# Reordering the beginning of a fused two-block transformer kernel: transfers in another order, a first group of six output tiles, and the lent PSUM banks given to a group's last tiles

## The reference

```python
# first block, for l in 0, 1 (stages 0 to 3)
h = concat(meta_tokens, x)                          # 272 x 1024
u = rms_norm(h, norm_mix_pre[l])
a_q, a_k, a_v, b_q, ..., gates = split(u @ w_in[l]) # 1024 -> 8416 columns
o_a = diff_attention(a_q, a_k, a_v, ..., rel_bias_table)   # four branches
o_b, o_c, o_d = gated linear attention, latent attention, windowed attention (also rel_bias_table)
merged = sum over branches of (o @ w_branch) * sigmoid(gates)
h = h + rms_norm(merged @ w_out[l], norm_mix_post[l])
h = h + rms_norm(conv_ffn(rms_norm(h, norm_ffn_pre[l])), norm_ffn_post[l])
# second block (stages 4 to 10)
x = x + 0.5 * swiglu_ffn(x, ...)      # stage 4, then 6, 7, 9
x = x + mixer(x)                      # stage 5: retention and dilated; stage 8: stick-breaking
return rms_norm(x, final_norm)
```

## Time and profile before

| | |
|---|---|
| median of 3 runs | 2211.29 us (2211.26 to 2211.96) |
| the profiled execution, its own time | 2209.07 us |
| its span | 2207.3 us |
| TensorE busy with matmuls | 2168.1 us, 98% of the span |
| VectorE busy | 1513.9 us, 69% |
| ScalarE busy | 1195.3 us, 54% |
| GpSimd busy | 293.4 us, 13% |
| granted TensorE clock, mean over the span | 0.998 |

### The profile page before, as it was taken

The page is one execution under the profiler, slowest core; times in us unless marked ns, Lnnn a source line. Parts: engine busy times, 40 slices in busy tenths (PEclk is TensorE's granted clock), DMA queues, the critical chain, the costliest instruction groups (busy, mean ns, idle before and its releaser), DMA issues.

```text
span 2207.3 us, 43398 instructions
## 1 busy us (share of the span) xinstructions
PE 2168.1 (98%) x17591; PEld 2086.1 (95%) x17591; DVE 1513.9 (69%) x2614; ACT 1195.3 (54%) x2053; POOL 293.4 (13%) x273
## 2 busy tenths in 40 slices
PE   7999999999999999999999999999999999999998
PEld 6989989999998999899999999889999999989998
DVE  5776676887478576779856665677665665886654
ACT  4555456665546555566655444455445444665443
POOL 1000112000110001220002220002210220232211
PEclk9999999999999999999999999999999999999999
DMA  7334435455643354454554655335555555435554
GB/s 239 113 128 139 134 115 177 130 178 173 216 124 115 115 151 135 129 181 154 184 196 175 210 185 186 125 124 174 189 184 182 190 183 187 149 123 170 185 187 128
DMA packets 97815, 356.61 MB, mean 162 GB/s; under 512 B 10848, under 2 KB 12000, under 8 KB 97488
## 3 DMA queue, kind: packets, MB, share of 16 engines
q1 hardware_dynamic: 95328, 342.47, 47.9%
q0 software_dynamic: 2000, 10.38, 1.7%
q10 hardware_dynamic: 288, 0.99, 0.1%
HBM read 352.68 MB, written 1.12 MB: 160 GB/s over the span
## 4 chain that ended last, share of the span: by engine, by line
PE 88%; DVE 7%; ACT 3%; issue 1%; DMA 1%; POOL 0%; SPq 0%; DVEq 0%; ACTq 0%; POOLq 0%
PE pd L1335 26%; PE pd L1346 25%; PE pd L1343 25%; DVE wlo L2211 2%; PE pt L1479 1%; DMA raw<-in_w 1%; PE pd L1495 1%; ACT whi L1786 1%; PE ps L1335 1%; PE ps L1343 1%; PE ps L1346 1%; PE ps L1454 1%; PE ps L1688 1%; PE pd L1601 1%; PE pd L1509 1%
## 5 line engine op out<-in xcount | busy, mean ns | idle before, releaser
L1335 PE MATMUL pd<-xh,whi 128*128 128x256 f32 (+2 forms) x3352 | 981.5, 293 | 1.5 <-DVE tb L2732 1.1
L1786 ACT ACTIVATE whi<-raw 128x1024 fp32r<-128x1024 f32 x618 | 651.2, 1055 | 597.0 <-PE pd L1346 569.6
L1346 PE MATMUL pd<-xh,wlo 128*128 128x256 f32 (+2 forms) x3343 | 950.0, 284 | 6.0 <-DVE wlo L2211 6.0
L2211 DVE TENSOR_TENSOR wlo<-raw,whi 128x1024 fp32r<-128x1024 f32 x618 | 769.5, 1246 | 266.0 <-ACT whi L1786 264.1
L1343 PE MATMUL pd<-xl,whi 128*128 128x256 f32 (+2 forms) x3343 | 948.8, 284 | 0.0
L1335 PEld LDWEIGHTS pd<-xh,whi 128*128 128x128 f32 x3352 | 633.4, 189 | 25.9 <-issue 18.7
L1346 PEld LDWEIGHTS pd<-xh,wlo 128*128 128x128 f32 x3343 | 631.6, 189 | 7.3 <-DVE wlo L2211 7.3
L1343 PEld LDWEIGHTS pd<-xl,whi 128*128 128x128 f32 x3343 | 630.1, 188 | 2.6
L1346 PE MATMUL pd<-ah,wlo 128*128 128x256 f32 (+1 forms) x992 | 280.7, 283 | 0.0
L1343 PE MATMUL pd<-al,whi 128*128 128x256 f32 (+1 forms) x992 | 279.7, 282 | 0.0
L1335 PE MATMUL pd<-ah,whi 128*128 128x256 f32 (+1 forms) x992 | 279.4, 282 | 0.0
(11 more groups left out here) (368 smaller groups left out, 3008.9 us busy)
## 6 DMA issues: line engine op xcount, KB each, us to landing
raw<-in_w SPq DMA_DIRECT2D x648, 512.0 KB, 3.5
TA<-scr POOLq DMA_DIRECT2D x2, 1392.0 KB, 10.4
C<-in_c POOLq DMA_DIRECT2D x1, 2432.0 KB, 11.7
TD<-scr POOLq DMA_DIRECT2D x2, 1056.0 KB, 7.7
TD<-scr POOLq DMA_DIRECT2D x2, 768.0 KB, 12.9
h<-in_h SPq DMA_DIRECT2D x4, 272.0 KB, 7.5
out<-u SPq DMA_DIRECT2D x8, 128.0 KB, 1.8
C<-in_c POOLq DMA_DIRECT2D x1, 800.0 KB, 5.5
```

Source lines behind the costliest of these rows:

```text
L1335: e.matmul(out, hi, xh, start=begin, stop=False)
L1346: last = e.matmul(out, lo, xh, start=False, stop=end)
L1786: e.activation(m.whi[i][:, 0:n], m.raw[c % NRAW][:, 0:n], ACT.Copy).then_inc(*self.up("ac_hi", ("hi", c)))
L2211: e.tensor_tensor(m.wlo[i][:, 0:n], m.raw[c % NRAW][:, 0:n], m.whi[i][:, 0:n].bitcast(F32), ALU.subtract).then_inc(*self.up("dv_lo", ("lo" ...
```

## The change

Five things are edited.

1. **Order of the first transfers.** SyncE issues chunk 0, `h` parts 0 and 1, chunk 1, `h` parts 2 and 3, chunk 2 and so on (`load_h`). ScalarE issues `C0` and only the first 16 columns of the gains (`FIRST_GAINS`, the gains of stage 0's norm); the other 1534 columns are issued as a step of its list, `load_gains`, at -1.8, which is behind the first `x_hi`. ScalarE and VectorE wait for the first part only at their start, and for the rest at a step `gains` at 2.0. GpSimd issues `btab` when chunk 0 has landed.
2. **x behind the first chunk, squares later.** x_hi and x_lo for k = 0, 1 are placed ahead of chunk 1's split, those for k = 2 to 7 behind it. The squares of `h` go to 0.5 to 2.6, the sum and root from 1.6 to 4.2.
3. **The bias table later.** `bias` goes from ahead of chunk 0 to 1.2 and 1.6, into bank `pt`; the rest of its chain follows (store at 2.5, the constants C1 at 2.9). `fill` at the start is three float32 matmuls of 388 columns on `C0` and waits for no weights.
4. **First group of six tiles** in stage 0, three of them in lent banks (before: three tiles, none lent).
5. **Lent banks for the last tiles of a group**, not the first. This matters where a group has six tiles: stages 0, 2 and 4. And `first` is kept to stages 0 to 4, so that stages 6, 7 and 9 run their first blocks in the plain order.

```diff
@@ Plan.dense
-            self.hold("px" if i < lent else "pd", t.begin, t.end + 0.4, t.key)
+            self.hold("px" if i >= len(tiles) - lent else "pd", t.begin, t.end + 0.4, t.key)
@@ Plan.await_root
-        self.first.update(t.key for t in tiles)
+        if tiles[0].key[0] <= 4:
+            self.first.update(t.key for t in tiles)
@@ Plan.mixer
-        n = 6 if l else 3
-        self.await_root(self.dense(qk[:n], True, 3 if l else 0))
-        self.dense(qk[n:])
+        self.await_root(self.dense(qk[:6], True, 3))
+        self.dense(qk[6:])
...
-            self.bias_tables(c0 - 1.5)
+            self.bias_tables(c0 + 1.2)
@@ Plan.bias_tables
+        self.step("pe", -0.01, "fill", 0)
         self.step("gp", t - 20, "load_btab")
-        self.step("gp", t + 1, "load_c1")
+        self.step("gp", t + 1.7, "load_c1")
         for i in range(2):
-            self.hold("pd", t + 0.1 * i, t + 0.1 * i + 0.3, ("bias", i))
-            self.step("pe", t + 0.1 * i, "bias", i)
-            self.step("dv", t + 0.1 * i + 0.2, "bias_out", i)
-        self.step("pe", -0.01, "fill", 0)
-        self.step("dv", t + 0.5, "bias_mask")
-        self.step("gp", t + 0.6, "store_bias")
+            self.hold("pt", t + 0.4 * i, t + 0.4 * i + 0.35, ("bias", i))
+            self.step("pe", t + 0.4 * i, "bias", i)
+            self.step("dv", t + 0.4 * i + 0.15, "bias_out", i)
+        self.step("dv", t + 1.2, "bias_mask")
+        self.step("gp", t + 1.3, "store_bias")
@@ make_plan
+    for i in range(4):
+        p.step("sp", (0.1, 0.2, 1.1, 1.2)[i], "load_h", i)
     for k in range(8):
-        p.split_x(0, k, -0.6 + 0.05 * k, False)
-        p.squares(-1, k, -0.59 + 0.05 * k, "h")
-    p.norm_root(0, 1.6)
+        p.step("ac", (-1.82 if k < 2 else -0.8) + 0.05 * k, "x_hi", 0, k)
+        p.step("dv", (-1.25 if k < 2 else -0.28) + 0.05 * k, "x_lo", 0, k)
+        p.squares(-1, k, 0.5 + 0.3 * k, "h")
+    p.step("ac", -1.8, "load_gains")
+    for engine in ("ac", "dv"):
+        p.step(engine, 2.0, "gains")
+    p.norm_root(0, 4.2)
@@ Tensor.fill
         if c == 0:
-            for s in self.ahead(("c0",), ("gains",)):
-                e.wait_ge(*s)
-            e.matmul(bank, m.c0("ident"), m.G[:, 0:512], start=True, stop=True)
+            for _ in range(3):
+                e.matmul(bank[:, 0:m.C0.shape[1]], m.c0("ident"), m.C0, start=True, stop=True)
+            return
@@ Scalar.run
-        e.dma_start(m.G, m.io["gains"]).then_inc(*up("gains", ("gains",), by=16))
+        e.dma_start(m.G[:, 0:FIRST_GAINS], m.io["gains"][:, 0:FIRST_GAINS]).then_inc(*up("gain0", ("gain0",), by=16))
@@ Pool.load_btab
+        for s in self.ahead(("raw", 0)):
+            self.e.wait_ge(*s)
```

More of the change, by code:

```diff
@@ L23 @@
 BIG = 1e30
+FIRST_GAINS = 16
 LNEXP = "natural_log_exp_and_others"
@@ L1123, in buf, with gains @@
         return self.m.ring[ring][self.p.buf[ring, key]]
+    def gains(self):
+        for s in self.ahead(("gains",)):
+            self.e.wait_ge(*s)
     def free(self, ring, key):
@@ L1377, in fill @@
             e.wait_ge(*s)
-        for _ in range(10 if c else 3):
+        for _ in range(10):
             e.matmul(bank, w[:, 0:128], w[:, 0:512], start=True, stop=True)
@@ L1439, in bias @@
         a, n = BIAS_CUTS[i]
-        for s in self.ahead(("btab",), ("gains",), self.free("pd", ("bias", i))):
+        for s in self.ahead(("btab",), ("gains",), self.free("pt", ("bias", i))):
             e.wait_ge(*s)
-        e.matmul(self.buf("pd", ("bias", i))[0:16, 0:n], m.gain("table", 0)[0:32, :], m.btab[0:32, 0, a:a + n],
+        e.matmul(self.buf("pt", ("bias", i))[0:16, 0:n], m.gain("table", 0)[0:32, :], m.btab[0:32, 0, a:a + n],
                  start=True, stop=True).then_inc(*self.up("pe_small", ("bias", i)))
@@ L1749, in run @@
         steps = {
-            "hi": self.hi, "table": self.table, "norm_rs": self.norm_rs,
+            "hi": self.hi, "table": self.table, "load_gains": self.load_gains, "gains": self.gains, "norm_rs": self.norm_rs,
             "x_hi": self.x_hi, "z_hi": self.z_hi, "y_sq": self.y_sq, "y_out": self.y_out, "h_sq": self.h_sq,
@@ L1769, in run @@
             e.wait_ge(*s)
-        for s in self.ahead(("gains",)):
+        for s in self.ahead(("gain0",)):
             e.wait_ge(*s)
@@ L1773, in run, with load_gains @@
             steps[name](*args)
+    def load_gains(self):
+        self.e.dma_start(self.m.G[:, FIRST_GAINS:], self.m.io["gains"][:, FIRST_GAINS:]).then_inc(
+            *self.up("gains", ("gains",), by=16))
     def table(self):
@@ L2179, in run @@
         steps = {
-            "lo": self.lo, "x_lo": self.x_lo, "z_norm": self.z_norm, "z_lo": self.z_lo, "post_mul": self.post_mul,
+            "lo": self.lo, "gains": self.gains, "x_lo": self.x_lo, "z_norm": self.z_norm, "z_lo": self.z_lo, "post_mul": self.post_mul,
             "post_add": self.post_add, "copy_out": self.copy_out, "scaled_out": self.scaled_out, "gate_in": self.gate_in,
@@ L2671, in bias_out @@
             e.wait_ge(*s)
-        e.tensor_copy(self.m.tabs[0:16, 0, a:a + n], self.buf("pd", ("bias", i))[0:16, 0:n]).then_inc(
-            *self.up("dv_out", ("bias_out", i), ("free", "pd", ("bias", i))))
+        e.tensor_copy(self.m.tabs[0:16, 0, a:a + n], self.buf("pt", ("bias", i))[0:16, 0:n]).then_inc(
+            *self.up("dv_out", ("bias_out", i), ("free", "pt", ("bias", i))))
     def bias_mask(self):
@@ L3047, in run, with load_h @@
     def run(self):
-        e, m = self.e, self.m
-        for i in range(4):
-            e.dma_start(m.h[:, 2 * i:2 * i + 2, :], m.io["h0"][:, 2 * i:2 * i + 2, :]).then_inc(
-                *self.up(f"h{i}", ("h", 0, 2 * i), ("h", 0, 2 * i + 1), by=16))
+        e = self.e
+        steps = {"load": self.load, "load_h": self.load_h, "store": self.store}
         for _, _, name, args in self.p.steps["sp"]:
-            if name == "load":
-                self.load(*args)
-            else:
-                self.store(*args)
+            steps[name](*args)
         for s in self.ahead(("stored",)):
             e.wait_ge(*s)
+    def load_h(self, i):
+        h = slice(2 * i, 2 * i + 2)
+        self.e.dma_start(self.m.h[:, h, :], self.m.io["h0"][:, h, :]).then_inc(
+            *self.up(f"h{i}", ("h", 0, 2 * i), ("h", 0, 2 * i + 1), by=16))
     def load(self, c):
```

1 line of the change is left out of this document (added).

## The result

| | before | after |
|---|---|---|
| median of 20 runs each, us | 2210.59 (2208.35 to 2212.01) | 2207.29 (2205.42 to 2211.78) |
| profiled execution, own time / span, us | 2209.07 / 2207.3 | 2207.68 / 2205.9 |
| mean granted clock of that execution | 0.998 | 0.996 |

The ratio is 0.9986 (95% interval 0.998 to 0.9992): the change makes the kernel 3.3 us faster by the medians, 3.1 by the ratio. That is a real gain, under half of the 7.2 us forecast, and it lies within the 0.2% that the prediction called "same". The time is just at the end of the forecast's range.

What follows compares the result with a forecast made beforehand. TensorE, busy 2168.1 of 2207.3 us, was taken as the bound. Chunk 6 starting at 30.1 instead of 37.30 gains 7.2 us, later stages nothing: 2211.3 - 7.2 = 2204.1 us, range 2200.9 to 2207.3.

Steps and rivals of the forecast that it cites:

- same: Whole kernel: a change within about 0.2% (4.4 us), which a measurement can't tell from none; chance 0.11.
- Dense work: Start: fill and splits arrive together, first dense matmul at 8.6 us, 5.7 us earlier than 14.28.
- the copy into TA: Rival "Slower": TA's copy delays chunk 8's load; TA issued at 32.5 gives 2214.8, forecast assumed 23 to 24; chance 0.03.
- Stage 4's bank wait: Stage 4: the 1.08 us bank wait goes, but the wlo wait grows from 0.52 to 1.60; zero in all.
- landing at 14.0, a wait of 0.7 us: Chunk 1: the gains, issued at 7.3, take 6.7 us and land at 14.0; the bias matmul waits 0.7 us.
- 0.95 for both bias matmuls: Chunk 1: the two bias matmuls cost 0.95 us on the path; chunk 2 then starts at 17.2.
- The clock falls once more: Rival: waits at the bias matmul or in stage 4 bring half clock; gain 5.5 us, 2205.8; chance 0.12.
- The argument against it: Against the clock rival: the 2.20 us stall at 20.96 in the kernel before had no half clock behind it.
- Ends: 0 and 1.08; I take 0: Stage 4: bounds of the gain from the lost bank wait, 0 to 1.08 us; forecast took 0.
- which costs 1.7 us: Stage 2: price of 3.4 us at half clock (708.80 to 712.20) behind a 1.83 us stall.
- the first rival: "More is won": quick start, early gains, or stage 4's 1.08 stays; gain 8 to 10 us, 2201.3 to 2203.3; chance 0.15.
- the 11.2 of the rival: Start: the 16 gains columns in 64-byte pieces land late, like a row of 11.2 us; 2209.1; late transfers together 0.13.

Runs made afterwards that it cites:

- experiment 7: Kernel before with only the lent banks moved to a group's last tiles: median 2212.14 us, ratio 1.0005 to before.
- 9: Changed kernel with the bias table one chunk later and lent banks back at a group's first tiles: median 2203.28 us, ratio 0.9969 to before.
- experiment 2: Changed kernel with the bias matmuls and their chain one chunk later (2.2 instead of 1.2): median 2203.84 us, ratio 0.9971 to before.
- 10: Changed kernel with the bulk of the gains issued at the program's start, not behind the first split: median 2204.88 us, ratio 0.9976 to before.
- experiment 3: Changed kernel with nine unread 512-column matmuls ahead of the first bias matmul, filling its wait: median 2204.72 us, ratio 0.9977 to before.
- experiment 1: The changed kernel once more, unedited, as control: median 2208.37 us, ratio 0.9991 to before.
- experiment 4: Changed kernel with the lent banks back at a group's first tiles: median 2206.0 us, ratio 0.998 to before.
- experiment 5: Changed kernel with the wlo split of stage 4's ninth chunk moved forward on VectorE: median 2205.95 us, ratio 0.998 to before.
- experiment 6: Changed kernel with the bias table one chunk later and stage 4's late wlo split moved forward: median 2202.64 us, ratio 0.9964 to before.
- 8: Experiment 6 with a wlo split in stage 2 brought forward too: median 2203.14 us, ratio 0.9965 to before.

## Why the prediction was wrong in size

**Right.** Dense work at 8.63 (forecast 8.6), where two errors cancel by luck: C0 landed at 5.16 instead of 4.8, and the fill took 3.47 us instead of 3.8; chunk 1 at 12.19 (12.5); the stalls for wlo and acc gone; weights in time, though the copy into TA was issued only at 28.16 instead of 23 to 24: ScalarE waited for chunks (2.49 and 1.50 us, near 40), TensorE did not. Stage 4's bank wait turned into one wait for wlo, 1.86 us against the 1.60 forecast, for no gain: experiments 7 and 9 and the table bear the zero out, as long as the clock holds.

**The first step that failed: "landing at 14.0, a wait of 0.7 us".** The gains were issued 1.3 us earlier than I put it, at 6.04, but took 8.9 us and not 6.7: they landed at 15.0, and the wait is 2.01. I had judged 7.7 us of before as the price of heavier company; beside the raw chunks and btab it was no less. At chunk 2 that is 1.1 us (the first bias matmul at 15.12 against 14.0). The forecast had 0.95 for both bias matmuls; the first alone took that (15.12 to 16.07), and the second adds 0.26.

**The second, "The clock falls once more" at 0.12.** It was a rival and should have been the forecast. The six blocks of chunk 1 behind the wait took 20.24 - 16.07 - 0.26 = 3.91 us instead of 2.27, so 1.64 more. 17.2 + 1.1 + 0.26 + 1.64 is 20.2, where chunk 2 is; the same 3.0 to 3.1 us stand between forecast and chunk 6 (33.16 against 30.1). The experiments show this cause: without the wait (2, and 10) or with the wait filled (3) the clock stays at 1.00. In all four traces that have the open wait for the gains (after, 1, 4, 5; 2.01, 2.35, 1.67 and 1.62 us) the clock falls behind it: 0.50, 0.51, 0.59 in 16 to 19.4 of experiment 4, 0.50 in 19 to 21 of experiment 5. None of the six without it (2, 3, 6, 8, 9, 10) has a slow stretch there. The argument against it, that the 2.20 us stall at 20.96 had no such follow-up, rested on one case in one execution; in experiment 7 the same stall has it.

The twelve traces together, counted from their time lines and clock rows (the profiles before and after, and ten experiments):

```
place                                  idle before, us   traces with it   slow stretch behind
start, gains                           1.62 to 2.35       4               4
start, wlo of chunk 1 (order before)   2.20, 2.21         2               1  (7)
stage 2, wlo, near 705                 1.83, 1.84        11               9  (not 1, 5)
stage 4, merged wait, near 1200        1.84 to 1.86       6               3  (after, 2, 7)
near 1485, DVE RG                      1.59, 1.60        12               0
near 163, small matmuls                none              12               7  (after, 1, 3, 4, 5, 7, 9)
near 752, small matmuls                none              12               2  (1, 5)
near 768, small matmuls                0.57              12               1  (1)
```

So 17 of 23 open waits of 1.6 to 2.4 us for the gains or for wlo are followed by a fall, and none of the twelve near 1485. At 0.12 the rival was priced far too low.

**The third, stage 4's "Ends: 0 and 1.08; I take 0".** It had no end below nothing. The merged wait of stage 4 was followed by the lower clock in three of the six traces that have it (after, 2, 7; not 1, 3, 10), and costs 1.5 us then, by the table. Two waits of 1.08 and 0.52 were not followed by it (before, 4, 9). The Trainium skill (TensorE: Matmul & The Clock Gate, HAM oscillation) has waits for data put the array back to half clock, in an example with DMA waits of about 3 to 5 us. These traces agree, already for waits of 1.6 to 2.4 us, but not in every execution and not at every place. The rival's price, "which costs 1.7 us" in stage 2, was wrong for its own place: there the slow stretch costs nothing (experiment 1).

**The sizes add up.** Forecast 7.2; measured 3.3 by the medians and 1.4 by the two profiled executions. Of the latter's 5.8 us: 3.1 lost at the start, 1.07 behind small matmuls near 163 (4.14 to 3.07), 1.55 in stage 4, 0.1 after. With the bias matmuls where the gains have landed the change is worth 6.8, close to the 7.2. The lower end of the forecast's range, 2200.9, is not what it was said to be: the middle of the first rival is 2202.3. The lower clock also shows in the runs without a trace. The changed kernel's 20 executions have mean granted clocks of 0.995 (2), 0.996 (12) and 0.997 (6), with median times of 2210.9, 2207.3 and 2205.6; 21 of before have 0.997 (10), 0.998 (10) and 0.999 (1), at 2211.5, 2209.5 and 2208.3. A stretch of 3.4 us at half clock is 0.0008 of such a mean.

**Open.** Why the clock fell in one execution and not in another at the same place, and why never near 1485. Whether the small matmuls near 163 can be kept from a fall was not tried. All five traces with a slow stretch at the beginning (after, 1, 4, 5, 7) have the one near 163 too, and two of the other seven (3, 9): the two may hang together, so the 1.07 us may be a late part of the same price, but no run separates them. In experiment 6 the sum came out 1 us or more short. A part is the start: its trace has waits of 0.34 and 0.74 us for the splits of chunk 2, and chunk 6 at 31.58, 0.85 later than in experiment 2; the rest is not settled. Which of the other parts of the change (the order of h and the chunks, the later squares, the group of six) earns how much of the gain was not tested.

## What to carry to other kernels

When a change moves work that needs a late transfer into dense work, don't price the landing under the slowest like transfer of the trace (7.7 us here, and it took 8.9), and put the consumer behind it with a margin of a chunk; if it can't be moved, give the engine something to do in the wait. Price a wait of TensorE of about 2 us at the wait plus, more often than not, the slow stretch behind it (1.5 us in stage 4, 1.6 at the start), and expect one merged wait to be dearer than two short ones of the same sum. But look first whether another engine sets the pace there, since a slow stretch costs nothing where later waits shrink by as much, and look at more than one execution: one trace without a fall proves little. "In the order of need" is worth testing transfer by transfer: the one that was kept back here didn't need to be.

## What the runs showed of the hardware

- TensorE falls to 1.2 GHz for 3.4 us behind a single wait of 1.6 to 2.4 us in work that is otherwise dense, in 17 of 23 cases; once for 6.8 us (experiment 1). A wait of 1.6 us near 1485 has no fall behind it in any of twelve traces. Nine matmuls that fill 2 us of the wait for the gains keep it at 1.00 (experiment 3). A fall can also stand behind small matmuls without idle time (162.5 to 166: clock 0.54), in 7 of 12 traces.
- What a slow stretch of 3.4 us costs: 1.5 us in stage 4 (180.85 against 179.33), 1.64 at the start, nothing in stage 2 (5.58 with and without it).
- 767 KB issued at 1.67 took 6.9 us to land, issued at 6.04 they took 8.9. 8 KB in pieces of 64 bytes took 4.7 us beside 512 KB loads, far from the 11.2 of the rival.
